# One launch of a hybrid decoder step: the value product of decode attention by page strips instead of head strips

## The reference

```python
def diff_attn_block(q, k, v, q_pos, k_pos, lam, subln_w, lam_init):
    s = jnp.einsum('bqhd,bkhd->bhqk', q, k).astype(jnp.float32) * (DH_C ** -0.5)
    ...
    p = jax.nn.softmax(s, axis=-1)
    B, _, Tq, Tk = p.shape
    p = p.reshape(B, H_C, 2, Tq, Tk)
    attn = p[:, :, 0] - lam * p[:, :, 1]
    o = jnp.einsum('bhqk,bkhe->bqhe', attn.astype(v.dtype), v)
    o = rms_norm(o, subln_w, SUBLN_EPS) * (1.0 - lam_init)
    return o.reshape(B, Tq, D_C)

k_past = cache_k[l, page_table].reshape(Bd, past_len, 2 * H_C, DH_C)
v_past = cache_v[l, page_table].reshape(Bd, past_len, H_C, 2 * DH_C)
```

## Time and profile before

| What | Value |
|---|---|
| Median of 3 runs | 4049.2 us (4043.1 to 4051.12) |
| Profiled execution, its own time | 4044.38 us |
| Span of the profiled execution, first to last instruction | 4042.6 us |
| Mean granted clock of TensorE | 0.946 |
| Busy shares: TensorE, weight loads, VectorE, ScalarE, GpSimd | 91%, 85%, 39%, 29%, 9% |
| DMA | 352.84 MB, mean 87 GB/s |

### The profile page before, as it was taken

How to read it: one execution, slowest core, us unless ns; L and a number is a source line. 1 busy time by engine, 2 the same in 40 slices (tenths; PEclk the granted TensorE clock), 3 DMA queues, 4 the chain that set the end, 5 groups by cost and what they waited for, 6 DMA issues and landing times. The chain is left out here.

```text
span 4042.6 us, 81476 instructions
## 1 busy us (share of the span) xinstructions
PE 3667.5 (91%) x32956; PEld 3439.9 (85%) x32956; DVE 1566.5 (39%) x2280; ACT 1156.3 (29%) x1829; POOL 369.9 (9%) x602
## 2 busy tenths in 40 slices
PE   6999899888899988999989998997888998989997
PEld 5999898756877788999989997986687777989997
DVE  4332423523544454333343334244244444543333
ACT  2222222333332342222232222133323233322222
POOL 0000003300233200000000000033002331000000
PEclk9999999978999999999989999998889899999998
DMA  2232323372211152222222323234621111422322
GB/s 78 74 87 80 94 74 105 100 260 88 63 33 33 30 167 68 83 83 83 63 79 76 88 76 90 83 107 138 229 73 46 33 44 59 153 65 73 88 77 66
DMA packets 524937, 352.84 MB, mean 87 GB/s; under 512 B 33314, under 2 KB 474572, under 8 KB 523954
## 3 DMA queue, kind: packets, MB, share of 16 engines
q1 hardware_dynamic: 503214, 342.64, 27.8%
q10 hardware_dynamic: 21508, 7.28, 0.7%
HBM read 321.34 MB, written 28.51 MB: 87 GB/s over the span
## 5 line engine op out<-in xcount | busy, mean ns | idle before, releaser
L299 PE MATMUL dense<-h_hi,whi 128*128 128x288 f32 x4032 | 1205.0, 299 | 64.9 <-DVE h_lo L445 58.0
L300 PE MATMUL dense<-h_lo,whi 128*128 128x288 f32 x4032 | 1196.5, 297 | 0.0
L301 PE MATMUL dense<-h_hi,wlo 128*128 128x288 f32 x4032 | 1191.9, 296 | 0.0
L283 DVE TENSOR_TENSOR wlo<-raw,whi 128x1024 fp32r<-128x1024 f32 (+1 forms) x444 | 518.0, 1167 | 1388.1 <-ACT whi L279 1387.9
L279 ACT ACTIVATE whi<-raw 128x1024 fp32r<-128x1024 f32 (+1 forms) x444 | 450.1, 1015 | 1528.8 <-PE dense L301 1457.1
L299 PEld LDWEIGHTS dense<-h_hi,whi 128*128 128x128 f32 x4032 | 761.6, 189 | 72.7 <-issue 60.4
L301 PEld LDWEIGHTS dense<-h_hi,wlo 128*128 128x128 f32 x4032 | 766.3, 190 | 0.0
L300 PEld LDWEIGHTS dense<-h_lo,whi 128*128 128x128 f32 x4032 | 763.9, 189 | 0.0
L299 PE MATMUL dense<-ffn_a_hi,whi 128*128 128x288 f32 x1408 | 416.8, 296 | 0.0
L300 PE MATMUL dense<-ffn_a_lo,whi 128*128 128x288 f32 x1408 | 415.4, 295 | 0.0
L301 PE MATMUL dense<-ffn_a_hi,wlo 128*128 128x288 f32 x1408 | 413.9, 294 | 0.0
(11 more groups left out here) (343 smaller groups left out, 4796.9 us busy)
## 6 DMA issues: line engine op xcount, KB each, us to landing
raw<-in_w_in_dram SPq DMA_DIRECT2D x124, 512.0 KB, 3.9
raw<-in_ffn_w_gate_dram SPq DMA_DIRECT2D x88, 512.0 KB, 3.8
raw<-in_ffn_w_up_dram SPq DMA_DIRECT2D x88, 512.0 KB, 3.8
page<-in_cache_v_dram SPq DMA_DIRECT2D x128, 256.0 KB, 5.5
raw<-in_ffn_w_down_dram SPq DMA_DIRECT2D x64, 384.0 KB, 3.3
page<-in_cache_k_dram SPq DMA_DIRECT2D x96, 256.0 KB, 4.0
raw<-in_ffn_w_down_dram SPq DMA_DIRECT2D x64, 320.0 KB, 3.2
merge_gate<-gates_scratch SPq DMA_DIRECT2D x16, 864.0 KB, 5.2
```

Of the source, the lines that this page charges most:

```text
L283: dve.tensor_tensor(self.wlo[s][:, 0:n, :], self.raw[s][:, 0:n, :], self.whi[s][:, 0:n, :].bitcast(F32), ALU.subtract)\
L299: pe.matmul(o, w_hi, hi[:, c, t], start=(first and c == 0), stop=False)
L300: pe.matmul(o, w_hi, lo[:, c, t], start=False, stop=False)
L301: mm = pe.matmul(o, w_lo, hi[:, c, t], start=False, stop=(last and c == chunks - 1))
```

## The change

Three things are done in the stage, all in `sample_attention`:

1. The value product has one matmul per page, with all 512 value columns moving. Page j writes strip j mod 4, so a strip collects the partial sums of two pages (three for strip 0: pages 0 and 4 and the new tokens).
2. `rows` grows from 128 to 512 columns and the copy to it with it.
3. On the way back the transpose is replaced by four matmuls, one per head: that head's 128 columns of `rows` are the stationary operand and 8 columns of a new constant `pick` move. `pick` is the sum of the four 32-column strips of the identity, so that these matmuls add the four strips, pick the head's 8 rows and transpose. `pick` is made by three VectorE additions at the start of the stage, after the wait for the tables; TensorE's program of the stage begins with a wait for it.

```diff
-        rows = tile("rows", [P, P])
+        rows = tile("rows", [P, HC * P])
+        pick = tile("pick", [P, HC * TS])
...
             @block.tensor
             def _(pe):
+                V.wait(pe, "pick")
                 with pe.Fori(0, NB // NU) as t:
...
                     def back(u):
                         At.wait(pe, f"rows{u}", t)
-                        Qt.did(pe.transpose(self.D[1][:, 1, 0:P], rows[:], self.ident[:]), f"back{u}")
+                        for h in range(HC):
+                            mm = pe.matmul(self.D[1][:, 1, h * TS:(h + 1) * TS], rows[:, h * P:(h + 1) * P],
+                                           pick[:, h * TS:(h + 1) * TS], start=True, stop=True)
+                        Qt.did(mm, f"back{u}")
...
-                            for h in range(HC):
-                                mm = pe.matmul(self.E[1][strip(h), 1, 0:P], at[0:m, j * n_at:(j + 1) * n_at],
-                                               v[:, h * P:(h + 1) * P], start=(j == 0), stop=(j == NPG))
+                            mm = pe.matmul(self.E[1][strip(j % 4), 1, :], at[0:m, j * n_at:(j + 1) * n_at], v,
+                                           start=(j < 4), stop=(j + 4 > NPG))
...
-                        own = self.D[1][:, 1, 0:HC * (n_at + TS)].rearrange("p (h x) -> p h x", h=HC)[:, :, 0:TS]
+                        own = self.D[1][:, 1, 0:HC * TS].rearrange("p (h x) -> p h x", h=HC)
...
-                        At.did(act.activation(rows[:], self.E[1][:, 1, 0:P], ACT.Copy), f"rows{u}")
+                        At.did(act.activation(rows[:], self.E[1][:, 1, :], ACT.Copy), f"rows{u}")
...
                 dve.wait_ge(tables, 48)
 
                 V.own(dve)
+                V.did(dve.tensor_tensor(pick[:], self.ident[:, 0:32], self.ident[:, 32:64], ALU.add))
+                for n in (2, 3):
+                    V.own(dve)
+                    V.did(dve.tensor_tensor(pick[:], pick[:], self.ident[:, strip(n)], ALU.add), "pick" if n == 3 else None)
                 V.did(dve.scalar_tensor_tensor(e0[:], comb[:, 1, :], self.nlam[:], comb[:, 0, :], ALU.mult, ALU.add))
```

## The result

| | before | changed |
|---|---|---|
| Median | 4047.4 us (6 runs, 4043.1 to 4052.2) | 4075.1 us (6 runs, 4069.7 to 4077.1) |
| Profiled execution, own time and span | 4044.4, 4042.6 us | 4076.8, 4075.0 us |

The account below looks back on a forecast made before the run. TensorE, busy 91% of the span, was taken to bound the kernel, its chain with VectorE and ScalarE setting the stage. Mid-turn exponentials, ways back, turns' ends and start summed to +39 on 4044.4, so 4083, range 4067 to 4099.

Parts of the forecast that it names:

- the bounds named ahead: Forecast is wrong if the stage's stretch grows under 14 or over 25 us per layer, or some difference lies outside it.
- The product: Value product on TensorE: fullest strip goes from 2304 to 3072 columns, +0.65 us, +1.3 at clock 0.50; removed loads give nothing.
- The copy: ScalarE's copy `rows` out of PSUM: 512 columns take 0.597 us where 128 took 0.28, +0.32 us.
- the cover of 0.52: Mid-turn, the exponential started 0.52 us after ScalarE's copy `rows` ended, time that hides part of a longer product and copy.
- The way back: `back` on TensorE: one transpose becomes eight records paying full weight loads, +0.77 us each time, +1.5 at clock 0.50.
- The start: Start of each layer's stage: TensorE waits for `pick`, 4.7 us late; first copy and scores 4.0 late, 8.0 for both layers.
- `pv(3)`, `rows`, `back(3)` in series at 0.50, four times: End of each turn, nothing covered, at the lower clock: four times 1.3 + 0.32 + 1.5, 12.5 us.
- rival 1: Upper clock in the turn's end: terms 0.4 and 1.74 in place of 1.3 and 3.1, -9, so 4074; chance 0.08.
- the 1.3 of the sum: `back(2)` before `pv(3)` at clock 0.50, partly beside the copy to `at`: four times 1.3, 5.2 us.
- Rival 4: The longer turn's end carries clock 0.50 into the following weights' turn or scores: 4090 to 4100; chance 0.06.
- rival 5: Faster through the clock: most of the two stages' 104 us at 0.50 vanish, result 4030; chance 0.03.

Follow-up runs that it names:

- e2: Changed kernel with the new tokens' product split by head over the four strips (four matmuls of 128 columns for one of 512): 4070.4 us, ratio 1.0066.
- e9: Kernel before with only ScalarE's copy of the product's bank widened from 128 to 512 columns: 4048.5 us, ratio 1.0000.
- e3: Kernel before with only the way back changed, four matmuls of 8 moving columns in place of one transpose: 4062.7 us, ratio 1.0040.
- e4: Kernel before with only a wait added: TensorE's first transpose waits for the VectorE operation behind the table loads. 4045.3 us, ratio 1.0001.
- e7: Kernel before with the way back's one transpose moved into TensorE's idle time, except the turn's last: 4035.5 us, ratio 0.9967.
- e10: Kernel before with unused matmuls, their result never read, in two of TensorE's idle times: 4022.2 us, ratio 0.9936.
- e6: Changed kernel with `pick` made before the tables, new tokens split by head over the strips, and twelve of sixteen ways back moved into idle time: 4039.5 us, ratio 0.9982.
- e8: Changed kernel with pages in the order 0, 4, 1, 5, 2, 6, 3, 7, so two products in a row write one strip: 4077.8 us, ratio 1.0071.

## Why the prediction was right

The forecast was 4083, from a sum of +39 on the profiled execution; that execution now took 4076.8 (+32), the median is 4075.1 (+27.7). The profiled execution had the lowest granted clock of the six, 0.943 where the others had 0.945 or 0.946. Sign, range and most of the mechanisms held, and so did the bounds named ahead: 17.0 and 18.6 us a stage, between 14 and 25, and no growth outside it. Two errors of 7 to 8 us each, below, went opposite ways.

- *The product*: +0.65 forecast at the upper clock, 2.79 - 2.21 = 0.58 measured. That the loads are hidden and the fullest strip's columns count was shown from both sides: pages' product 39.6 and 38.4 us, and e2.
- *The copy*: 0.597 measured in all 16, and the cover of 0.52 was as read. Alone it was free (e9), behind the longer product it delayed the exponential by 0.38 us, where the forecast had 0.45.
- *The way back*: +0.77 forecast, 1.06 - 0.33 = 0.73 measured; at the lower clock +1.5 and 1.88 - 0.48 = 1.40. The Trainium skill (TensorEngine Tiling (Array Packing), Instruction Overhead) states some 60 cycles as the overhead of a matmul. The trace doesn't agree for a stationary operand of 128 float32 columns: a record costs 0.12 us at the upper clock (0.99 us for eight in e3), and in e3 the launch pays 15 us, not the 4 that this rule would leave as an estimate. The forecast's sum by that rule was also slightly off: with 0.2 us at the upper clock and 0.35 at the lower in its own terms it is about 4070, not 4073.
- *The start*: TensorE 4.8 and 5.0 late (4.7 forecast), the first key copy 4.1 (4.0 forecast), the scores 3.2 and 3.7 late (4.0 forecast). The last part was too high because more of the key transposes fell behind the clock's rise: from the first transpose to the scores the granted clock was 0.74, where it was 0.54, and from the first key copy to the scores it took 6.45 us, where it was 7.37.
- *The step that was off* is the last term, "`pv(3)`, `rows`, `back(3)` in series at 0.50, four times", 12.5 us. The clock there didn't stay. `back(3)` ran at the upper level in all four turns, the product's end too: from `pv(3)`'s start to the next keys' the first turn took 881.32 - 875.99 = 5.33 before and 891.56 - 885.34 = 6.22 now, +0.9 and not +3.1. The other three ends grew by 1.1 to 1.3 (the last of each layer taken to the first square), so the four together cost 4.6 us and not 12.5. That is the mechanism of rival 1, whose 4074 is 1 us from the median, though only its second half: before `pv(3)` the lower clock stayed, and `back(2)` cost 1.2 (883.53 to 885.34, against 0.62 before), the 1.3 of the sum.
- *What the sum didn't have* is more of the lower clock in the middle of the turns. The scores took 9.2 us more of TensorE, the weights' turn 2.7 less. Rival 4 had named more low clock, but carried over from the longer turn's end, and that isn't what the rows show: the scores at 854.80 run at 3.48 before any turn has ended, and the first scores behind a turn's end (898.96) take 1.93 as before. Low time in the two stages rose from 122 to 142 us, some 7 us of time at 0.33. That this nearly made up for the turns' ends is luck. (The stage is 139 us long, not the stretch of 124 that the forecast read, so its 104 us at the lower clock in rival 5 were 122.)
- *What the forecast treated as fixed and isn't*: the clock's low stretches move when anything ahead of them moves. e4 shows a delay of 2.8 us per layer that cost the launch nothing as it was timed and some 4 to 5 us at equal clock, e7 a saving of 2 to 4 that brings 13, e10 pure filling that brings 26.

Open: what places the low stretches. The runs show that filling TensorE's idle times lifts the clock, and that the profile with the start shifted by 2.8 us had less low time too; a rule by which one could have computed 47 in place of 61 us wasn't found. For the runs that weren't profiled only the granted clock of the whole launch is known, not where in it the low time lies.

## What to carry to other kernels

Before trading many narrow matmuls for few wide ones, count the moving columns of the fullest strip, not instructions: with eight pages and the new tokens in four strips, a quarter of the matmuls took more time. A small matmul with a full float32 stationary operand costs 0.11 to 0.12 us a record at the upper clock, whether it moves 8 columns or 32, so look where it stands in the chain; with twelve of sixteen moved into idle time (e6) little of that cost was left. And where a stage's clock is below 1.00, price a change at both clocks, compare kernels at equal low time, and try filling TensorE's idle times first: here that brought 26 us, twice what the best rearrangement did, until the pages' DMA became the next limit.

## What the runs showed of the hardware that wasn't expected

- Products for the same strip, one behind the other in the program, overlap with the others' as well as if they alternated: e8's sixteen records of 512 columns take 1.94 us against 1.89, with two neighbours always in one strip.
- Unused matmuls, 28 records a stage, made the stage 10.4 us shorter, with TensorE's clock at 0.92 in place of 0.78.
- A microsecond at the lower clock costs 0.26 to 0.36 us of this stage, and 0.37 us over the 64 launches of the kernel before; that the rest is covered by the chain through the other engines is argued, not shown.
